# Block one's attention: scores issued two units ahead, behind the transposes, and a shorter VectorE chain

## The chip, the cores and the metric

The kernel runs on one core of one Trainium2 chip. The metric is the device time of one launch in microseconds (us). The engines named below are TensorE (PE in the profile, with PEld for its weight loads), VectorE (DVE), ScalarE (ACT), GpSimd (POOL) and SyncE (SP), which issues the weight loads from HBM.

## The reference

Two stacks of two layers each work on 256 tokens with 1024 channels. The change is in the first stack's token mixer. Each layer there has three kinds of softmax attention that a kernel computes side by side: compressed keys (15 of them, "cmp"), selected blocks and a sliding window (both over all earlier keys at this length, with a gate per head, "slc" and "win"), and attention with forget gates ("fox"). Cut to what the change touches:

```python
s_c = jnp.einsum('bqghd,bngd->bghqn', qb, kc)          # q was scaled by B_DH ** -0.5
p_c = _masked_softmax(s_c, cmp_end[None, :] <= t[:, None])

def _masked_softmax(logits, mask):
    m = jnp.max(logits, axis=-1, keepdims=True)
    p = jnp.where(mask, jnp.exp(logits - m), 0.0)
    return p / jnp.maximum(jnp.sum(p, axis=-1, keepdims=True), TINY)
# o = gate_cmp * o_cmp + gate_slc * o_slc + gate_win * o_win for the group heads; fox heads have no gate
```

The second stack (feed-forward layers, convolution, Fourier mixing and a latent attention) is untouched.

## The kernel before, in words

Nearly all of the time is weight products on TensorE. Weights stream from HBM through a ring of four slots; each 128x1024 tile is split in a high part (ScalarE, L773) and a low part (VectorE, L797), and three passes are made of it (L836, L840, L843).

The attention of block one is a stage of its own, once in each of the two layers, between the input products and the output product "wo". `units_block1` lists its 22 units: for each half of the queries (tt 0 and 1, 128 queries each) one cmp unit, then slc and win in turn four times, then two fox units. A unit is two heads. Its keys are 128 wide for tt 0 and 256 wide for tt 1. A unit has these steps, each with a semaphore that counts units:

- `unit_scores` (PE, L1114, or L1122/L1125 with a mask product L1131, for fox also L1130) writes two PSUM banks. It waits until the exponentials of the unit two before have been read out of those banks (`att_e`), and counts `att_s`.
- `unit_max` (DVE): two reductions L1201, a drain, and L1203 that writes the maximum negated and scaled; counts `att_m`. For cmp it is L1190 to L1196.
- `unit_exp` (ACT, L1254, L1249 for cmp): exponential with the row sum; counts `att_e`. It waits for the transposes of the unit two before, whose probability buffer it overwrites.
- `unit_norm` (DVE): reciprocal L1224, for slc and win the gate product L1228 with a drain, and two scalings of the probabilities L1232; counts `att_p`.
- `unit_turn` (PE, L1143, L1140 for cmp): transposes through the identity into bank 6; waits for `att_p` of its unit and for the copy of the unit before (`att_c`); counts `att_t`.
- `unit_copy` (ACT, L1266): bank 6 to SBUF; counts `att_c`.
- `unit_values` (PE, L1162, for slc also the compressed part L1156): values into bank 7; counts `att_v`. cmp has none.
- `unit_out` (ACT, L1273), for win and fox alone: bank 7 to SBUF; waits for `att_v`, counts `att_o`, for which the next slc or fox values wait.

Every engine takes its instructions in program order. In tick n PE does scores(n+1), one chunk of a modulation product ("ada", L934, in ticks 0 to 11 alone), turn(n-1) and values(n-2). DVE does max(n) and norm(n-1). ACT does exp(n), copy(n-1) and out(n-2). A few modulation steps (L915, L945, L955) lie between ticks. Behind the last out come the split of the attention output and the product wo.

Of the kernel before, what the change touches and what calls it, by code (L numbers as in the profile page):

```python
# [24 lines left out]
ALU = mybir.AluOpType  # L25
ACT = mybir.ActivationFunctionType
AX_X = mybir.AxisListType.X
# [10 lines left out]
DH = 64  # L38
# [527 lines left out]
def kernel_program(nc, streams, consts, params, x_cm, ctx_cm, out_cm, blocks=(1, 2)):  # L566
    with ExitStack() as stack:
# [100 lines left out]
        pr = pr_b.rearrange("p (u k) -> p u k", u=2)  # L668
# [12 lines left out]
        gate = gate_b.rearrange("p (t c) -> p t c", t=TT)  # L681
# [31 lines left out]
        s = Semaphores(sem)  # L713
# [361 lines left out]
        def units_block1(l):  # L1075
            out = []
            for tt in range(TT):
                out.append(Unit("cmp", tt))
                for g in range(2):
                    for j in range(2):  # L1080
                        out.append(Unit("slc", tt, g=g, j=j, first=True))
                        out.append(Unit("win", tt, g=g, j=j, last=True))
                for j in range(2):
                    out.append(Unit("fox", tt, j=j, first=True, last=True))
            base, obase = l * len(out), l * sum(x.last for x in out)
            vbase = l * sum(x.kind != "cmp" for x in out)
            o = v = 0
            for n, x in enumerate(out):
                x.u, x.o, x.v = base + n, obase + o, vbase + v
                x.kt = 1 if x.kind == "cmp" else x.tt + 1  # L1090
                x.keys = N_CMP if x.kind == "cmp" else x.kt * P
                x.scale = 1.0 if x.kind == "fox" else DH ** -0.5
                o += x.last
                v += x.kind != "cmp"
            return out
# [8 lines left out]
        def half_scores(x, hh):  # L1104
            return bank[(4, 5, 0, 2)[2 * (x.u % 2) + hh]]

        def unit_scores(pe, x):
            if x.u >= 2:
                pe.wait_ge(s.att_e, x.u - 1)
            q = slice(x.tt * P, (x.tt + 1) * P)  # L1110
            if x.kind == "cmp":
                for h in range(QH):
                    rows = slice(h % 2 * DH, h % 2 * DH + DH)
                    mm = pe.matmul(half_scores(x, h % 2)[:, h // 2 * N_CMP:(h // 2 + 1) * N_CMP], qr[rows, h // 2, q],  # L1114
                                   kcb[rows, h // 4 * N_CMP:(h // 4 + 1) * N_CMP], start=True, stop=True)
                mm.then_inc(s.att_s, 1)
                return
            for hh in range(2):
                rows = slice(hh * DH, hh * DH + DH)
                dst = half_scores(x, hh)[:, 0:x.keys]  # L1120
                if x.kind == "fox":
                    pe.matmul(dst, qkn[rows, 6 + x.j, q], qkn[rows, 8 + x.j, 0:x.keys], start=True, stop=False)  # L1122
                else:
                    key = kd[rows, x.g, 0 if x.kind == "slc" else 1, 0:x.keys]
                    pe.matmul(dst, qr[rows, 2 * x.g + x.j, q], key, start=True, stop=False)  # L1125
            for hh in range(2):
                dst = half_scores(x, hh)[:, 0:x.keys]
                if x.kind == "fox":
                    for st in range(x.kt):
                        pe.matmul(dst, fa[:, st, 2 * x.j + hh, q], gtk[:, st, 0:x.keys], start=False, stop=False)  # L1130
                mm = pe.matmul(dst[:, x.keys - P:x.keys], ident_b, causal_b, start=False, stop=True)  # L1131
            mm.then_inc(s.att_s, 1)
# [34 lines left out]

        def attention_pe(pe, l, units):
            unit_scores(pe, units[0])
            for n in range(len(units) + 2):  # L1170
                if n + 1 < len(units):
                    unit_scores(pe, units[n + 1])
                ada_pe(pe, l, TICK_ATT + n)
                if 1 <= n <= len(units):
                    unit_turn(pe, units[n - 1])
                if n >= 2:
                    unit_values(pe, units[n - 2])
                ada_fold_pe(pe, l, TICK_ATT + n)

        def unit_max(dve, x):  # L1180

            dve.wait_ge(s.att_s, x.u + 1)
            if x.u >= 2:
                dve.wait_ge(s.att_e, x.u - 1)
            if x.kind == "cmp":
                dst = c_sm[:, 0:heads_n].rearrange("p (h k) -> p h k", h=QH)
                pairs_of = c_sm[:, 0:heads_n].rearrange("p (m hh k) -> p m hh k", hh=2, k=N_CMP)
                for hh in range(2):
                    src = half_scores(x, hh)[:, 0:heads_n // 2].rearrange("p (m k) -> p m k", m=QH // 2)
                    dve.scalar_tensor_tensor(out=pairs_of[:, :, hh, :], in0=src, scalar=x.scale,  # L1190
                                             in1=cneg[:, x.tt, :].unsqueeze(1).broadcast_to([P, QH // 2, N_CMP]),
                                             op0=ALU.mult, op1=ALU.add)
                dve.drain()
                dve.tensor_reduce(c_max, dst, AX_X, ALU.max)
                dve.drain()
                dve.tensor_tensor(dst, dst, c_max.unsqueeze(2).broadcast_to([P, QH, N_CMP]),  # L1196
                                  ALU.subtract).then_inc(s.att_m, 1)
                return
            at = 2 * (x.u % 2)
            for hh in range(2):  # L1200
                dve.tensor_reduce(mx[:, at + hh:at + hh + 1], half_scores(x, hh)[:, 0:x.keys], AX_X, ALU.max)  # L1201
            dve.drain()
            dve.tensor_scalar(negmx[:, at:at + 2], mx[:, at:at + 2], -x.scale, None, ALU.mult).then_inc(s.att_m, 1)  # L1203

        def unit_norm(dve, x):

            dve.wait_ge(s.att_e, x.u + 1)
            at = 2 * (x.u % 2)
            if x.kind == "cmp":
                p_u = pr[:, x.u % 2, 0:heads_n].rearrange("p (h k) -> p h k", h=QH)  # L1210
                dve.tensor_tensor(p_u, p_u, cmask[:, x.tt, :].unsqueeze(1).broadcast_to([P, QH, N_CMP]), ALU.mult)
                dve.drain()
                dve.tensor_reduce(c_sum, p_u, AX_X, ALU.add)
                dve.drain()
                dve.tensor_scalar(c_sum, c_sum, TINY, None, ALU.max)
                dve.drain()
                dve.reciprocal(c_rcp, c_sum)
                dve.drain()
                dve.tensor_tensor(c_rcp, c_rcp, gate[:, x.tt, 0:QH], ALU.mult)
                dve.drain()  # L1220
                dve.tensor_tensor(p_u, p_u, c_rcp.unsqueeze(2).broadcast_to([P, QH, N_CMP]),
                                  ALU.mult).then_inc(s.att_p, 1)
                return
            dve.reciprocal(rcp[:, at:at + 2], smu[:, at:at + 2])  # L1224
            dve.drain()
            if x.kind != "fox":
                c0 = (8 if x.kind == "slc" else 16) + 4 * x.g + 2 * x.j
                dve.tensor_tensor(rcp[:, at:at + 2], rcp[:, at:at + 2], gate[:, x.tt, c0:c0 + 2], ALU.mult)  # L1228
                dve.drain()
            for hh in range(2):  # L1230
                c = slice(hh * x.keys, (hh + 1) * x.keys)
                last = dve.tensor_scalar(pr[:, x.u % 2, c], pr[:, x.u % 2, c], rcp[:, at + hh:at + hh + 1], None,  # L1232
                                         ALU.mult)
            last.then_inc(s.att_p, 1)

        def attention_dve(dve, l, units):
# [7 lines left out]
        def unit_exp(act, x):  # L1244
            act.wait_ge(s.att_m, x.u + 1)
            if x.u >= 2:
                act.wait_ge(s.att_t, x.u - 1)
            if x.kind == "cmp":
                act.activation(pr[:, x.u % 2, 0:heads_n], c_sm[:, 0:heads_n], ACT.Exp).then_inc(s.att_e, 1)  # L1249
                return  # L1250
            at = 2 * (x.u % 2)
            for hh in range(2):
                c = slice(hh * x.keys, (hh + 1) * x.keys)
                last = act.activation(pr[:, x.u % 2, c], half_scores(x, hh)[:, 0:x.keys], ACT.Exp, scale=x.scale,  # L1254
                                      bias=negmx[:, at + hh:at + hh + 1], accum_out=smu[:, at + hh:at + hh + 1])
            last.then_inc(s.att_e, 1)

# [675 lines left out]
        def block1_dve(dve, l):  # L1933
# [26 lines left out]

            dve.tensor_copy(qkg, param(f"qkg@{l}"))
            dve.drain()
            dve.tensor_scalar(qkg[:, 6:8], qkg[:, 6:8], DH ** -0.5, None, ALU.mult)
            dve.drain()
            dve.wait_ge(s.hn_rs, l + 1)
            for j in range(10):
# [1038 lines left out]
```

## Time and profile before

| | us |
|---|---|
| median of 3 runs | 2830.51 |
| lowest and highest | 2826.48, 2833.05 |
| profiled execution | 2829.12 |
| its span | 2827.3 |
| PE busy in it | 2741.4 (97%) |
| DVE busy in it | 1776.6 (63%) |
| ACT busy in it | 1065.5 (38%) |
| attention of layer 0, first to last weight load of the stage | 135.07 to 194.19 |
| attention of layer 1, the same | 529.43 to 588.16 |

The profile is one execution. Its own time is 1.8 us more than its span, which is from the first instruction to the last. A busy share says how much of the span an engine had an instruction in work. Ends of matmuls are modelled, so in the attention stage the start times of the weight loads (PEld) tell the order and pace of TensorE best.

### The profile page before, as it was taken

What the parts mean: (1) busy time and instruction counts of PE and PEld (TensorE: products, weight loads), DVE (VectorE), ACT (ScalarE), POOL (GpSimd) and SP (SyncE); (2) the same over time, 40 slices, a digit from 0 to 9 for tenths busy, and PEclk for the clock granted to TensorE, in tenths of its full rate; (3) what the DMA queues carried; (4) which work ended last, traced back from release to release, by engine and by line L of the source; (5) the groups of instructions that cost most, each with busy time, mean ns of one, the idle gap of its engine ahead of it and who ended that gap; (6) DMA issues with size and microseconds to landing.
All of it is one profiled execution on the core that took longest, in us unless ns stands there. A gap on an engine that the chain in (4) does not pass through costs nothing.

```text
span 2827.3 us, 45215 instructions
## 1 busy us (share of the span) xinstructions
PE 2741.4 (97%) x16508; PEld 2334.7 (83%) x16508; DVE 1776.6 (63%) x3023; ACT 1065.5 (38%) x1704; POOL 192.0 (7%) x184
## 2 busy tenths in 40 slices
PE   8999999999999999999999999999999999899998
PEld 8669999589988888775777788888788888689998
DVE  7466656566676565587675665555665557756665
ACT  5356444366342221325434322222322214554443
POOL 0000000000000000032213000000000000134000
PEclk9999999999999999999999999999999999999999
DMA  5535544635544433321432244433344433244554
GB/s 194 197 117 196 183 165 156 216 131 184 180 142 141 148 139 132 115 72 64 137 133 66 90 142 148 141 135 131 130 142 148 142 126 120 83 129 156 168 177 157
DMA packets 118649, 401.16 MB, mean 142 GB/s; under 512 B 12928, under 2 KB 20992, under 8 KB 118144
## 3 DMA queue, kind: packets, MB, share of 16 engines
q1 hardware_dynamic: 115408, 392.48, 41.0%
q10 hardware_dynamic: 3120, 7.07, 0.7%
q8 instruction: 76, 1.25, 0.2%
q14 instruction: 45, 0.37, 0.0%
HBM read 398.45 MB, written 1.05 MB: 141 GB/s over the span
## 4 chain that ended last, share of the span: by engine, by line
PE 86%; DVE 5%; issue 4%; DMA 2%; ACT 1%; POOL 1%; DVEq 1%; ACTq 0%; POOLq 0%; SPq 0%
PE bank L836 24%; PE bank L843 24%; PE bank L840 24%; PE bank L1595 2%; DMA ring<-weights 1%; PE bank L2088 1%; PE bank L2447 1%; PE bank L2444 1%; PE bank L2441 1%; DVE work L2209 1%; DVE hn_lo L1069 1%; PE bank L934 1%; DVE w_lo L797 1%; POOL w_lo L797 1%; PE bank L1326 1%
## 5 line engine op out<-in xcount | busy, mean ns | idle before, releaser
L773 ACT ACTIVATE w_hi<-ring 128x1024 fp32r<-128x1024 f32 (+1 forms) x548 | 572.1, 1045 | 1158.3 <-DMA ring<-weights 1157.7
L797 DVE TENSOR_TENSOR w_lo<-ring,w_hi 128x1024 fp32r<-128x1024 f32 (+1 forms) x538 | 658.9, 1226 | 526.6 <-ACT w_hi L773 522.1
L840 PE MATMUL bank<-hn_hi,w_hi 128*128 128x256 f32 (+1 forms) x2848 | 896.9, 333 | 0.0
L843 PE MATMUL bank<-hn_lo,w_hi 128*128 128x256 f32 (+1 forms) x2848 | 896.7, 333 | 0.0
L840 PEld LDWEIGHTS bank<-hn_hi,w_hi 128*128 128x128 f32 x2848 | 542.2, 190 | 52.2
L843 PEld LDWEIGHTS bank<-hn_lo,w_hi 128*128 128x128 f32 x2848 | 542.2, 190 | 52.1
L836 PE MATMUL bank<-hn_hi,w_lo 128*128 128x256 f32 (+1 forms) x2848 | 570.4, 336 | 10.3 <-DVE w_lo L797 7.3
L836 PEld LDWEIGHTS bank<-hn_hi,w_lo 128*128 128x128 f32 x2848 | 453.7, 190 | 71.3 <-issue 11.5
L840 PE MATMUL bank<-hid_hi,w_hi 128*128 128x512 f32 (+1 forms) x704 | 248.7, 362 | 0.0
L843 PE MATMUL bank<-hid_lo_a,w_hi 128*128 128x512 f32 (+1 forms) x640 | 226.2, 362 | 0.0
L964 DVE SCALAR_TENSOR_TENSOR conds<-ring,con 128x1024 f32<-128x1024 f32 x106 | 131.3, 1239 | 58.8 <-DMA ring<-weights 42.0
L836 PE MATMUL bank<-hid_hi,w_lo 128*128 128x512 f32 (+1 forms) x704 | 156.5, 363 | 0.0
L840 PEld LDWEIGHTS bank<-hid_hi,w_hi 128*128 128x128 f32 x704 | 132.9, 189 | 20.6
L836 PEld LDWEIGHTS bank<-hid_hi,w_lo 128*128 128x128 f32 x704 | 121.9, 189 | 20.7 <-DVE w_lo L797 0.2
L843 PEld LDWEIGHTS bank<-hid_lo_a,w_hi 128*128 128x128 f32 x640 | 120.8, 189 | 18.7
L966 DVE SCALAR_TENSOR_TENSOR ring<-ring,con 128x1024 f32<-128x1024 f32 x106 | 131.5, 1241 | 0.0
L840 PE MATMUL bank<-up_hi,w_hi 128*128 128x256 f32 x512 | 125.6, 283 | 0.0
L843 PE MATMUL bank<-up_lo,w_hi 128*128 128x256 f32 x512 | 125.6, 283 | 0.0
L2797 DVE SCALAR_TENSOR_TENSOR hid<-work,par,hid 128x512 f32<-128x512 f32 (+1 forms) x180 | 117.4, 707 | 4.8
L2861 POOL MEMSET work<- 128x1716 f32 x2 | 3.1, 1528 | 1492.4 <-issue 790.1
L840 PEld LDWEIGHTS bank<-up_hi,w_hi 128*128 128x128 f32 x512 | 98.3, 192 | 0.0
L843 PEld LDWEIGHTS bank<-up_lo,w_hi 128*128 128x128 f32 x512 | 98.3, 192 | 0.0
(350 smaller groups left out, 3127.7 us busy)
## 6 DMA issues: line engine op xcount, KB each, us to landing
ring<-weights SPq DMA_DIRECT2D x694, 512.0 KB, 3.3
ring<-weights SPq DMA_DIRECT2D x32, 384.0 KB, 3.0
ring<-weights SPq DMA_DIRECT2D x32, 256.0 KB, 2.9
ring<-weights SPq DMA_DIRECT2D x28, 192.0 KB, 2.3
con<-consts ACTq DMA_DIRECT2D x1, 2063.0 KB, 9.5
con<-consts ACTq DMA_DIRECT2D x1, 1088.0 KB, 5.4
res<-ctx_cm ACTq DMA_DIRECT2D x1, 1024.0 KB, 7.7
con<-params ACTq DMA_DIRECT2D x1, 1024.0 KB, 11.0
```

What stands on the lines that cost most here:

```text
L773: act.activation(w_hi[:, slot, 0:w], ring[slot][:, 0:w], ACT.Copy).then_inc(s.w_hi, 1)
L797: eng.tensor_tensor(w_lo[slot][:, 0:w], ring[slot][:, 0:w], w_hi[:, slot, 0:w].bitcast(F32), ALU.subtract).then_inc(s.w_lo, 1)
L836: pe.matmul(dst, w_lo[slot][:, k * P:(k + 1) * P], x_hi(k), start=(start and k == order[0]), stop=False)
L840: pe.matmul(dst, high, x_hi(k), start=False, stop=False)
L843: return pe.matmul(dst, high, x_lo(k), start=False, stop=(stop and k == order[-1]))
L934: mm = pe.matmul(ada_bank(h)[rows, :], cs[:, k, COND_AT - 2 * q:COND_W - 2 * q], ring[slot][:, i * 4 * P:(i + 1) * 4 * P], start=(q == 0 a ...
L964: dve.scalar_tensor_tensor(out=conds[:, :], in0=ring[slot][:, :], scalar=1.0, in1=crow[:, 0:D], op0=ALU.mult, op1=ALU.mult, accum_out=to[: ...
L966: dve.scalar_tensor_tensor(out=ring[slot][:, :], in0=ring[slot][:, :], scalar=1.0, in1=crow[:, D:2 * D], op0=ALU.mult, op1=ALU.mult, accum ...
L1069: last = dve.scalar_tensor_tensor(out=hn_lo[:, k, t], in0=sq[:, k, t], scalar=modulation(l)[:, SHIFT[which], k, c:c + 1], in1=hn_hi[:, k, ...
L1326: mm = pe.matmul(bank[6 + hh][:, c0:c0 + P], keys, queries, start=True, stop=True)
L1595: mm = pe.matmul(bank[2 * parity(lin, g)][:, q], sq[:, k, q], ring[slot_of(lin, g, 0)][:, k * P:(k + 1) * P], start=(k == 0), stop=(k == K ...
L2797: last = dve.scalar_tensor_tensor(out=dst, in0=src, scalar=taps[:, m, k:k + 1], in1=dst, op0=ALU.mult, op1=ALU.add)
```

## The change

Three things change. On TensorE the scores of a unit are issued two units ahead where they were issued one ahead, and their place in a tick moves from ahead of the ada chunk to between the transposes and the values. On VectorE the reduction itself writes the negated maximum, so that L1203 and one drain go; to this end the score scale moves into the query gain, and ScalarE's exponential loses its scale factor. And the gate of slc and win becomes a second factor of the two scalings, so that L1228 and its drain go. The first gain step (L1963) covers six columns instead of two.

```diff
         def attention_pe(pe, l, units):
             unit_scores(pe, units[0])
+            unit_scores(pe, units[1])
             for n in range(len(units) + 2):
-                if n + 1 < len(units):
-                    unit_scores(pe, units[n + 1])
                 ada_pe(pe, l, TICK_ATT + n)
                 if 1 <= n <= len(units):
                     unit_turn(pe, units[n - 1])
+                if n + 2 < len(units):
+                    unit_scores(pe, units[n + 2])
                 if n >= 2:
                     unit_values(pe, units[n - 2])
                 ada_fold_pe(pe, l, TICK_ATT + n)
...
             for hh in range(2):
-                dve.tensor_reduce(mx[:, at + hh:at + hh + 1], half_scores(x, hh)[:, 0:x.keys], AX_X, ALU.max)
-            dve.drain()
-            dve.tensor_scalar(negmx[:, at:at + 2], mx[:, at:at + 2], -x.scale, None, ALU.mult).then_inc(s.att_m, 1)
+                last = dve.tensor_reduce(negmx[:, at + hh:at + hh + 1], half_scores(x, hh)[:, 0:x.keys], AX_X, ALU.max,
+                                         negate=True)
+            last.then_inc(s.att_m, 1)
...
             dve.reciprocal(rcp[:, at:at + 2], smu[:, at:at + 2])
             dve.drain()
-            if x.kind != "fox":
-                c0 = (8 if x.kind == "slc" else 16) + 4 * x.g + 2 * x.j
-                dve.tensor_tensor(rcp[:, at:at + 2], rcp[:, at:at + 2], gate[:, x.tt, c0:c0 + 2], ALU.mult)
-                dve.drain()
             for hh in range(2):
                 c = slice(hh * x.keys, (hh + 1) * x.keys)
-                last = dve.tensor_scalar(pr[:, x.u % 2, c], pr[:, x.u % 2, c], rcp[:, at + hh:at + hh + 1], None,
-                                         ALU.mult)
+                share = rcp[:, at + hh:at + hh + 1]
+                if x.kind == "fox":
+                    last = dve.tensor_scalar(pr[:, x.u % 2, c], pr[:, x.u % 2, c], share, None, ALU.mult)
+                else:
+                    c0 = (8 if x.kind == "slc" else 16) + 4 * x.g + 2 * x.j + hh
+                    last = dve.tensor_scalar(pr[:, x.u % 2, c], pr[:, x.u % 2, c], share, gate[:, x.tt, c0:c0 + 1],
+                                             ALU.mult, ALU.mult)
             last.then_inc(s.att_p, 1)
...
-                last = act.activation(pr[:, x.u % 2, c], half_scores(x, hh)[:, 0:x.keys], ACT.Exp, scale=x.scale,
+                last = act.activation(pr[:, x.u % 2, c], half_scores(x, hh)[:, 0:x.keys], ACT.Exp,
                                       bias=negmx[:, at + hh:at + hh + 1], accum_out=smu[:, at + hh:at + hh + 1])
...
-            dve.tensor_scalar(qkg[:, 6:8], qkg[:, 6:8], DH ** -0.5, None, ALU.mult)
+            dve.tensor_scalar(qkg[:, 2:8], qkg[:, 2:8], DH ** -0.5, None, ALU.mult)
```

## Rows read from the trace of the kernel before

**Rows 1.** The page: busy time (share) by engine, and the chain that ended last.

```profile
PE 2741.4 (97%) x16508; PEld 2334.7 (83%) x16508; DVE 1776.6 (63%) x3023; ACT 1065.5 (38%) x1704; POOL 192.0 (7%) x184
PE 86%; DVE 5%; issue 4%; DMA 2%; ACT 1%; POOL 1%; DVEq 1%; ACTq 0%; POOLq 0%; SPq 0%
```

**Rows 2.** Stretches: length, PE, PEld, DVE, ACT, POOL busy (x), PEclk, DMA share, GB/s.

```profile
150.00:160.00 10.00, 10.00 (x74) 5.47 (x76) 4.47 (x25) 4.22 (x20) 0.00 (x0) 1.00 0.57 178
180.00:190.00 10.00, 9.79 (x74) 7.06 (x74) 5.16 (x22) 5.03 (x18) 0.00 (x0) 1.00 0.00 1
```

**Rows 3.** Timeline, layer 0, an ada tick: start, us, engine, line, out<-in [idle <-releaser].

```profile
146.52 0.20 PEld L1143 LDWEIGHTS bank<-con,work 128*128 128x128 f32 x2 [0.84 <-issue]
...
146.89 0.20 PEld L1162 LDWEIGHTS bank<-work 128*64 128x64 f32 x4 [0.17 <-issue]
...
147.26 0.30 PEld L1125 LDWEIGHTS bank<-hid 64*128 64x128 f32 x4 [0.17 <-issue]
...
147.90 0.14 PEld L934 LDWEIGHTS bank<-ring,conds 128*32 128x32 f32 x4
...
148.88 0.20 PEld L1143 LDWEIGHTS bank<-con,work 128*128 128x128 f32 x2 [0.84 <-issue]
```

**Rows 4.** Timeline, layer 0, one win tick of tt 1, PE's loads and ACT.

```profile
178.09 0.30 PEld L1125 LDWEIGHTS bank<-hid 64*128 64x128 f32 x4 [0.17 <-issue]
...
178.79 0.42 PEld L1143 LDWEIGHTS bank<-con,work 128*128 128x128 f32 x4
...
179.38 0.42 PEld L1162 LDWEIGHTS bank<-work 128*64 128x64 f32 x8 [0.17 <-issue]
...
179.49 0.60 ACT L1266 ACTIVATE work<-bank 128x512 f32<-128x512 f32 x1 [0.60 <-PE bank L1143]
...
179.97 0.30 PEld L1125 LDWEIGHTS bank<-hid 64*128 64x128 f32 x4 [0.17 <-issue]
...
180.09 0.28 ACT L1273 ACTIVATE work<-bank 128x128 f32<-128x128 f32 x1
...
180.26 0.47 ACT L1254 ACTIVATE work<-bank,small 128x256 f32<-128x256 f32 x1
...
181.06 0.21 ACT L1254 ACTIVATION_READ_ACCUMULATOR work<-bank,small 128x1 f32 x1
181.10 0.42 PEld L1143 LDWEIGHTS bank<-con,work 128*128 128x128 f32 x4 [0.38 <-DVE work L1232]
```

**Rows 5.** Timeline, layer 0, DVE in one slc tick of tt 1.

```profile
174.63 0.76 DVE L1201 TENSOR_REDUCE small<-bank 128x1 f32<-128x256 f32 x2
...
175.47 0.17 DVE L1203 TENSOR_SCALAR small<-small 128x2 f32<-128x2 f32 x1
...
175.78 0.16 DVE L1228 TENSOR_TENSOR small<-small 128x2 f32<-128x2 f32 x1
...
176.02 0.61 DVE L1232 TENSOR_SCALAR work<-work,small 128x256 f32<-128x256 f32 x2
```

**Rows 6.** Timeline, layer 0, fox scores of tt 1 and two waits of the tail.

```profile
182.49 0.30 PEld L1122 LDWEIGHTS bank<-hid 64*128 64x128 f32 x4 [0.17 <-issue]
...
185.08 0.42 PEld L1143 LDWEIGHTS bank<-con,work 128*128 128x128 f32 x4
...
190.91 0.66 PE L1143 MATMUL bank<-con,work 128*128 128x128 f32 x4 [0.60 <-DVE work L1232]
...
194.22 0.66 PE L1162 MATMUL bank<-work 128*64 128x128 f32 x8 [0.66 <-ACT work L1273]
```

**Rows 7.** Lines 1356 and 1358: one scaling with two factors, one with one.

```profile
L1356 DVE TENSOR_SCALAR work<-work,small x4: 406/408/414, 27.9 to 423.4; 128x256 f32<-128x256 f32 x4
L1358 DVE TENSOR_SCALAR work<-work,small x4: 345/346/349, 28.2 to 423.7; 128x256 f32<-128x256 f32 x4
```

**Rows 8.** Timeline, layer 1: first and last weight load of the attention.

```profile
529.43 1.00 PEld L1114 LDWEIGHTS bank<-small,hid 64*128 64x128 f32 x16 [2.33 <-issue]
...
588.16 0.45 PEld L1162 LDWEIGHTS bank<-work 128*64 128x64 f32 x8 [0.86 <-ACT work L1266]
```

More of the change, by code:

```diff
@@ L1091, in units_block1 @@
                 x.keys = N_CMP if x.kind == "cmp" else x.kt * P
-                x.scale = 1.0 if x.kind == "fox" else DH ** -0.5
                 o += x.last
@@ L1189, in unit_max @@
                     src = half_scores(x, hh)[:, 0:heads_n // 2].rearrange("p (m k) -> p m k", m=QH // 2)
-                    dve.scalar_tensor_tensor(out=pairs_of[:, :, hh, :], in0=src, scalar=x.scale,
+                    dve.scalar_tensor_tensor(out=pairs_of[:, :, hh, :], in0=src, scalar=1.0,
                                              in1=cneg[:, x.tt, :].unsqueeze(1).broadcast_to([P, QH // 2, N_CMP]),
```

## The prediction

> **What bounds the kernel now.** I read the page first, for the busy shares and the chain that ended last. TensorE is busy for 97% of the span and carries 86% of the chain [rows 1]. So an edit is worth what it does to TensorE's pace, and time saved on another engine is worth something only where TensorE waits for it. Next I read the stage, 135.07 to 194.19 in layer 0, by stretches: from 150 to 160 TensorE is busy all the time, from 180 to 190 for 9.79 of 10 us, with the clock at its full level (2.4 GHz) in both; the DMA engines are idle in the second stretch, so the ring is full and no weight is late [rows 2]. Whatever the stage gains or loses therefore passes on to wo. Last I read the timeline by the starts of weight loads. A tick with an ada chunk and without the compressed part lasts 2.36 us (146.52 to 148.88), of which the chunk holds PE for 0.98 (147.90 to 148.88) [rows 3]. A tt 1 tick without a chunk is scores 0.70 (178.09 to 178.79), transposes 0.59 (to 179.38) and values 0.59 (to 179.97), 1.88 in all [rows 4]; one with the compressed part has some 0.23 more, and fox scores last 2.59 (182.49 to 185.08) [rows 6]. TensorE's true waits are few: 0.38 for the scaling at 181.10 [rows 4], then 0.60 and 0.66 in the tail [rows 6].
>
> **VectorE's part.** L1203 starts at 175.47, 0.84 after the reductions, and L1224 follows it by 0.08; L1228 sits between at 175.78, and L1232 follows 0.24 behind it [rows 5]. The change takes away about 0.23 ahead of the exponential and 0.24 ahead of the scaling. The second factor adds time: 408 against 346 ns for the same size, 0.06 for each of two scalings [rows 7]. Net, VectorE has 0.35 us less in a slc or win unit. That the reduction costs the same with the sign turned no row shows; it is the same pass over the same elements, and I take nothing for it, between 0 and one L1203 (0.17, [rows 5]) in a unit. The two edits are worth what TensorE waited for VectorE. The gain on six columns and ScalarE's missing factor change no count and no width: 0, hidden in any case behind rows of 0.17.
>
> **How I sum the order of the work.** I laid the 22 units out. Each step starts at the later of its engine's turn and its semaphores: PE steps as above, an exponential of tt 1 takes 1.04 (180.26 to 181.06 and its second read of 0.21), a copy 0.60 with the next step 0.49 after its start, an out 0.28 with the next step 0.17 after (180.09 to 180.26); transposes release the copy 0.70 after they start (178.79 to 179.49), values release the out 0.71 after (179.38 to 180.09) [rows 4]. For the order before, this gives the last two waits in the right places (the transposes at 190.98, where the trace has 190.91 [rows 6]) and 59.6 us from the first scores to the end of the last values' issue; the trace has 135.07 to 194.22 and 0.42 for the eight loads. So it may be used for the order after, with an error of some 0.5 us.
>
> **What the move adds: tile switches.** PE's queue shows 0.17 of idle with no releaser whenever the shape of the array tile changes: 64 rows after values, 64 columns after transposes, and none between L1131 and the transposes, which both use the whole array [rows 3, 4]. In ticks 12 to 19, which have no chunk, the order scores, transposes, values has three changes (one lies inside the scores). The order transposes, scores, values has four. In chunk ticks both orders have five. With one around tick 13's fold I count 57 changes before and 66 after: 9 x 0.17 = 1.5 us a layer. The switches from transposes to scores and from the mask product to values are in no row; the bounds are 0 and 0.27 each. I take 0.17, since every other change shows it. The Trainium skill, TensorEngine Tiling (Array Packing), section Tiling Modes, states that a change of tiling mode drains TensorE. By that rule the move costs these switches, and without it none; the rows have it as the 0.17.
>
> **What the move adds: a wait.** Scores(n+2) write the banks of unit n, so they wait for exp(n). They used to be scores(n+1) waiting for exp(n-1), long done. Behind them on PE now stand values(n-2); for those stands out(n-2) on ScalarE; and behind out(n-2), in program order, exp(n+1), for which scores(n+3) wait. So where unit n-2 is win or fox there is a closed chain. Counting from the end of exp(n): scores 0.70, switch 0.17, values release the out at 0.87 + 0.71 = 1.58, exp(n+1) starts at 1.75 and ends at 1.75 + 1.04 = 2.79, 2.82 with its semaphore. PE meanwhile is through scores, values (0.87 + 0.59 = 1.46) and turn(n) (2.04), and then holds scores(n+3), with values behind them, for 0.78. In chunk ticks the 0.98 of the chunk covers this, and tt 0's exponential is shorter: 0.26 in one tick. Laid out over the stage, scores(14) wait 1.01 and scores(15) 1.25 (a modulation copy stands ahead of exp(13) as well), scores(18) and scores(20) 0.78 each: 3.8 us.
>
> **The sum.** Waits of PE before, by the same layout: 1.78 up to tick 18, the most for norm (0.40 and 0.50 behind cmp, 0.19, 0.25, 0.44), all but 0.28 of which the longer lead and the shorter VectorE chain remove; and 1.76 in the tail. After: 0.28 and 0.26 early, 3.82 for the exponentials, 1.96 in the tail, where scores(21) are delayed through out(17) and turn(20) waits 0.73. That is 6.3 against 4.0, +2.3 a layer; with the switches 1.5, +3.8. Layer 1 has the same stage (529.43 to 588.16, [rows 8]), so +7.7 us. The profiled execution has 2829.12 with a span of 2827.3; it would have 2836.8. That execution is 1.4 below the median of 2830.51, so on the median it is 2838.2, and I say 2838.
>
> **The rivals.** (a) *The outs don't bind, not slower.* If the values release the out before the scores matter, or the exponentials keep their lead, the 3.8 goes and the 1.3 that turn waited for norm stays won. Laid out with outs that never wait, the stage takes 58.7: -0.9 a layer, 2828.6. It speaks for it that in the 2.36 us ticks ScalarE has long pauses. It speaks against it that in tt 1 out and exponential follow within 0.17 [rows 4]. It decides where values plus out come less than 0.78 later than I have them. (b) *One of the two new switches is free.* 61.1 or 61.8 in place of 63.5: +1.5 or +2.1 a layer, 2833.4 to 2834.8. (c) *Both free and the outs don't bind, faster.* 55.3: -4.4 a layer, 2821.8; then TensorE's issue alone is the bound, and the 0.17 that rows show at other changes speaks against it. (d) *The new switches cost more*, 0.27: 66.6, +7 a layer, 2844.4. (e) That only VectorE's edits act, were the order without effect, gives 58.2 in the layout, -1.4 a layer, 2827.7; it is in (a)'s share.
>
> **How the numbers follow.** A measurement of this kernel can tell about 0.2%, 5.7 us, from no change. The forecast (both switches paid, closed chain) has 0.46; with 0.5 us for the layout's error either way and the same for the exponential's semaphore it holds +5.7 to +10. (b) has 0.25, (a) with (e) 0.14, (c) 0.06, (d) 0.09. Slower by over 0.2%: 0.46 + 0.09 = 0.55. Within: 0.25 + 0.14 = 0.39. Faster: 0.06. The range leaves out (c) and (d), 0.15 together, and runs from just under (a) to the top of the forecast with the spread of the medians: 2828 to 2842.
>
> **What would show it.** In the profile after: attention stages some 3.8 us longer each; in the tt 1 ticks PE idle before L1125 and L1122, released by ACT L1254, where before it was L1143 waiting for DVE L1232; L1273 of a tt 1 tick starting 1.4 or more after L1266 instead of 0.60; 0.17 of unreleased idle ahead of L1125 behind L1143, and ahead of L1162 or L1156 behind L1131; DVE with 40 fewer L1203 and 32 fewer L1228, and L1232 some 60 ns longer with two factors. The prediction is wrong if L1125 waits for nothing in ticks 12 to 19, or if the stage ends before 59 us.

## The result and the profile after

The changed kernel takes 2843.34 us (median of 7 runs, 2838.34 to 2847.35) against 2830.51 (7 runs): a ratio of 1.0043 with a 95% interval of 1.0029 to 1.0057, so 12.8 us slower. The direction was forecast; the size was 7.7, and the time lies 1.3 us above the range.

The page of the changed kernel, its busy times and the chain that ended last, to be read beside [rows 1]:

```profile
PE 2751.6 (97%) x16508; PEld 2341.4 (82%) x16508; DVE 1772.1 (62%) x2951; ACT 1067.0 (38%) x1704; POOL 191.8 (7%) x184
PE 86%; DVE 4%; issue 4%; ACT 2%; DMA 2%; POOL 1%; DVEq 1%; ACTq 0%; SPq 0%; POOLq 0%
```

TensorE has the same instructions and is busy 10 us longer; ScalarE's share of the chain has gone from 1% to 2%. VectorE has 72 instructions fewer. None of this tells where the time went. The two attention stages tell it, each from the first weight load of its scores to the end of the last one of its values (columns as in [rows 2]). First the two of the kernel before, by the same limits, then the two of the changed kernel:

```profile
135.07:194.64 59.57, 56.55 (x438) 32.47 (x438) 37.21 (x166) 32.53 (x119) 0.00 (x0) 1.00 0.40 141
529.43:588.61 59.18, 56.64 (x438) 32.46 (x438) 37.16 (x166) 32.62 (x119) 0.00 (x0) 1.00 0.40 138
138.73:205.41 66.68, 60.85 (x438) 34.63 (x438) 34.28 (x130) 31.68 (x119) 0.00 (x0) 0.95 0.36 123
541.25:607.37 66.12, 59.34 (x438) 32.93 (x438) 34.12 (x130) 31.76 (x119) 0.00 (x0) 0.97 0.36 124
```

The stages of the changed kernel are 7.1 and 6.9 us longer. The span is 16.6 longer in this execution; 3.7 of it lie ahead of the first stage (its start was 135.07), where the order of the attention plays no part yet; I put them down to the scatter of single executions. The forecast had +3.9 a stage. The third column from the right shows what comes on top: the mean granted clock is 0.95 and 0.97 of full, where the stages before had 1.00. Half of the time spent at half speed is lost, so 0.05 x 66.68 = 3.3 us were lost to the clock in the first stage, and 0.03 x 66.12 = 2.0 us in the second. The first stage without that is 63.4 us long; the layout by hand had 63.5.

The second stage is another case. Its loads wait for weights in the first ticks, the clock is low right behind that wait, and it is full again from 552 to the end of the stage:

```profile
547.90 0.14 PEld L934 LDWEIGHTS bank<-ring,conds 128*32 128x32 f32 x4 [1.47 <-DMA ring<-weights]
```

```profile
548.00:550.00 2.00, 2.00 (x8) 0.37 (x8) 0.00 (x0) 0.00 (x0) 0.00 (x0) 0.59 0.71 277
550.00:552.00 2.00, 2.00 (x11) 0.80 (x10) 0.79 (x4) 1.08 (x5) 0.00 (x0) 0.56 0.72 229
```

That stretch lies ahead of ticks 12 and 13 and is not behind the waits described next. It also comes in executions of versions that are not slower (see the experiments), so the 6.9 us of this stage are not all owed to the change.

The waits are where they were forecast, in both layers. Layer 0, ticks 12 and 13, TensorE's weight loads:

```profile
172.16 0.14 PEld L1139 LDWEIGHTS bank<-con,work 128*120 128x120 f32 x1 [0.17 <-DVE work L1221]
173.52 0.30 PEld L1124 LDWEIGHTS bank<-hid 64*128 64x128 f32 x4 [1.22 <-ACT work L1255]
...
174.37 0.20 PEld L1161 LDWEIGHTS bank<-work 128*64 128x64 f32 x4
174.74 0.42 PEld L1142 LDWEIGHTS bank<-con,work 128*128 128x128 f32 x4 [0.17 <-issue]
176.58 0.51 PEld L1124 LDWEIGHTS bank<-hid 64*128 64x128 f32 x4 [1.43 <-ACT work L1255]
```

The scores L1124 wait 1.22 and 1.43 for the exponential L1255 (1.01 and 1.25 were forecast, besides the switch of 0.17). In the last row a group of four loads takes 0.51 where it took 0.30 three rows above. The clock in these microseconds:

```profile
176.00:178.00 2.00, 1.42 (x7) 0.77 (x7) 0.90 (x3) 1.93 (x8) 0.00 (x0) 0.58 0.00 0
178.00:180.00 2.00, 2.00 (x12) 2.00 (x11) 0.21 (x3) 0.00 (x0) 0.00 (x0) 0.50 0.00 0
180.00:182.00 2.00, 2.00 (x11) 1.02 (x9) 1.62 (x8) 1.26 (x4) 0.00 (x0) 0.50 0.00 0
```

TensorE stood still for two waits of over a microsecond close together. From about 176.2, within the second wait, it was granted the lower of its two levels (1.2 GHz), and kept it until about 183, though it was busy all the time from 178 to 182. The closed chain is seen best in tick 16 (layer 0, TensorE's loads and ScalarE's steps):

```profile
184.04 0.30 PEld L1124 LDWEIGHTS bank<-hid 64*128 64x128 f32 x4 [0.17 <-issue]
...
184.89 0.41 PEld L1161 LDWEIGHTS bank<-work 128*64 128x64 f32 x8
...
185.47 0.42 PEld L1142 LDWEIGHTS bank<-con,work 128*128 128x128 f32 x4 [0.17 <-issue]
...
185.59 0.28 ACT L1274 ACTIVATE work<-bank 128x128 f32<-128x128 f32 x1 [0.85 <-PE bank L1161]
185.77 0.47 ACT L1255 ACTIVATE work<-bank,small 128x256 f32<-128x256 f32 x1
...
186.83 0.30 PEld L1124 LDWEIGHTS bank<-hid 64*128 64x128 f32 x4 [0.94 <-ACT work L1255]
```

Scores at 184.04, values behind them at 184.89, the out L1274 0.70 later after 0.85 of idling on ScalarE, the exponential behind it, and 0.94 of waiting before the next scores. VectorE's edits came out as read from [rows 5, 7]. These are groups of the changed kernel (count, busy us, mean ns, idle before): the reduction costs the 352 ns of before with its sign turned; the two-factor scaling L1233 is 377 on the average of both widths, against 317 for the one-factor form.

```profile
L1201 DVE TENSOR_REDUCE small<-bank 128x1 f32<-128x128 f32 (+1 forms) x80 | 24.8, 352 | 29.7 <-PE bank L1130 29.7
L1233 DVE TENSOR_SCALAR work<-work,small 128x128 f32<-128x128 f32 (+1 forms) x64 | 21.4, 377 | 2.5
L1230 DVE TENSOR_SCALAR work<-work,small 128x128 f32<-128x128 f32 (+1 forms) x16 | 4.4, 317 | 0.6
```

### The profile page after: what moved, and what is told of

Read it like the earlier page. It is cut to its first block, busy times and chain, and to the rows that moved or that the text cites. A ratio compares the mean times of both kernels' runs of the same rounds, so it can differ in the third digit from the quotient of the medians.

```text
span 2843.9 us, 45071 instructions
## 1 busy us (share of the span) xinstructions
PE 2751.6 (97%) x16508; PEld 2341.4 (82%) x16508; DVE 1772.1 (62%) x2951; ACT 1067.0 (38%) x1704; POOL 191.8 (7%) x184
## 3 DMA queue, kind: packets, MB, share of 16 engines
q8 instruction: 76, 1.25, 0.2%
## 4 chain that ended last, share of the span: by engine, by line
PE 86%; DVE 4%; issue 4%; ACT 2%; DMA 2%; POOL 1%; DVEq 1%; ACTq 0%; SPq 0%; POOLq 0%
PE bank L836 24%; PE bank L843 24%; PE bank L840 24%; PE bank L1596 2%; DMA ring<-weights 2%; PE bank L2089 1%; PE bank L2448 1%; PE bank L2442 1%; PE bank L2445 1%; DVE work L2210 1%; DVE hn_lo L1069 1%; PE bank L934 1%; POOL w_lo L797 1%; PE bank L1327 1%; PE bank L2118 1%
## 6 DMA issues: line engine op xcount, KB each, us to landing
con<-consts ACTq DMA_DIRECT2D x1, 2063.0 KB, 10.2
```

## The experiments

The theory (A) is that the order of TensorE's work makes a closed chain of waits, and that the clock falls behind these waits. In short diffs the changed kernel is the one being edited unless it says otherwise.

**One part alone: VectorE's edits.** The scores go back to one ahead, ahead of the chunk; the rest of the change stays.

```diff
-            unit_scores(pe, units[1])
             for n in range(len(units) + 2):
+                if n + 1 < len(units):
+                    unit_scores(pe, units[n + 1])
                 ada_pe(pe, l, TICK_ATT + n)
...
-                if n + 2 < len(units):
-                    unit_scores(pe, units[n + 2])
```

> VectorE's two edits alone, with the scores one ahead and in their old place. Theory A (the loss is the order of TensorE's work): the stage shrinks from 59.6 to about 58.2 us in each layer, and the kernel takes 2.8 us less than the one before, with L1203's drain and L1228's gone and two-factor scalings some 60 ns longer. Rival B (the loss comes from the shorter VectorE chain, for instance from the reductions that write the sign turned): slower than before, by up to the 12.8 us of the whole change.

Measured: 2828.83 (11 runs) against 2831.56 (29), ratio 0.9992 (0.9983 to 1.0000): 2.7 us less, at the edge of what can be told from nothing. The stages:

```profile
137.21:195.46 58.25, 56.01 (x438) 32.43 (x438) 33.70 (x130) 32.37 (x119) 0.00 (x0) 1.00 0.42 144
531.17:592.01 60.84, 57.67 (x438) 32.79 (x438) 33.54 (x130) 32.38 (x119) 0.00 (x0) 0.97 0.40 135
```

The first is the 58.2 of the layout. The second has a wait of 1.6 us for weights in its first ticks and a short stretch of lower clock right behind it (0.03 x 60.84 = 1.8 us), as the second stage of the changed kernel had. B is out: VectorE's part does not cost time.

**The other part alone: the order.** The kernel before, with TensorE's order of the change.

> The new order of TensorE alone, with VectorE's steps as before. Theory A: 63.6 us a stage where the clock stays full, as waits of about 1.2 and 1.4 us before the scores of ticks 12 and 13 and of about 0.9 in ticks 16 and 18; +8 us from these alone, and with the clock falling behind them in some executions +8 to +14 against before. Rival B: about the time of before.

Measured: 2844.12 (5 runs), ratio 1.0045 (1.0032 to 1.0058), 12.6 us more: the whole loss. Its first stage is 66.68 us long, with 6.8 us at half speed behind tick 13. Its second stage:

```profile
537.09:604.97 67.88, 62.14 (x438) 35.19 (x438) 37.74 (x166) 31.91 (x119) 0.00 (x0) 0.92 0.35 120
...
572.00:574.00 2.00, 1.62 (x14) 0.77 (x12) 1.57 (x6) 0.92 (x3) 0.00 (x0) 1.00 0.00 0
574.00:576.00 2.00, 1.19 (x5) 0.54 (x6) 0.94 (x4) 2.00 (x9) 0.00 (x0) 0.53 0.02 4
576.00:578.00 2.00, 2.00 (x13) 2.00 (x12) 0.00 (x0) 0.16 (x2) 0.00 (x0) 0.50 0.04 8
```

Here the clock fell at 574, in the second of the two waits, and stayed down for 10.2 us; half of that, 5.1 us, went with it, and the stage without them is 62.8 long.

**The chain opened on TensorE.** The scores stay two ahead, behind the values.

```diff
+                if n >= 2:
+                    unit_values(pe, units[n - 2])
                 if n + 2 < len(units):
                     unit_scores(pe, units[n + 2])
-                if n >= 2:
-                    unit_values(pe, units[n - 2])
```

> The whole change, but the scores two ahead stand behind the values in each tick, not ahead of them. Theory A (scores, values, out and the next exponential form a closed chain, and a ninth more tile switches): the chain is open and the switches are those of before, so a stage takes 58.2 us, -2.8 against before and some -15 against the changed kernel, and TensorE waits nowhere for an exponential over 0.3 us. Rival C (having scores two ahead at all is what costs, since the banks are those of the unit whose exponential is not done): the waits for the exponentials stay and the time is that of the changed kernel, +12.

Measured: 2827.50 (12 runs), ratio 0.9989 (0.9980 to 0.9998): 4.1 us under the kernel before and some 16 under the changed one. Both stages are 57.7 us long, at full clock:

```profile
136.47:194.16 57.69, 56.08 (x438) 32.33 (x438) 33.50 (x130) 32.33 (x119) 0.00 (x0) 1.00 0.41 141
528.94:586.64 57.70, 56.09 (x438) 32.33 (x438) 33.52 (x130) 32.34 (x119) 0.00 (x0) 1.00 0.40 141
```

And a tick of its timeline (TensorE's loads, ScalarE's steps):

```profile
175.52 0.42 PEld L1161 LDWEIGHTS bank<-work 128*64 128x64 f32 x8 [0.17 <-issue]
176.11 0.30 PEld L1124 LDWEIGHTS bank<-hid 64*128 64x128 f32 x4 [0.17 <-issue]
176.22 0.28 ACT L1274 ACTIVATE work<-bank 128x128 f32<-128x128 f32 x1
176.40 0.47 ACT L1255 ACTIVATE work<-bank,small 128x256 f32<-128x256 f32 x1
...
176.81 0.42 PEld L1142 LDWEIGHTS bank<-con,work 128*128 128x128 f32 x4
```

The out L1274 starts 0.70 after the values as ever, but the scores run beside it, and the transposes follow the mask product L1130 with no switch. C is out: two ahead is not in itself what costs.

**The chain opened on ScalarE.** TensorE's order is the change's, but the copy of a finished output stands behind the next exponential.

```diff
                     unit_exp(act, units[n])
+                if 3 <= n <= len(units):
+                    unit_out(act, units[n - 3])
                 if 1 <= n <= len(units):
                     unit_copy(act, units[n - 1])
-                if n >= 2:
+                if n >= len(units):
                     unit_out(act, units[n - 2])
```

> The changed kernel, with ScalarE's copy of a finished output put behind the next exponential, not ahead of it; TensorE's order is as in the change. Theory A: the exponential no longer stands behind the values, the waits of ticks 12 to 19 go, and a stage takes 59.0 us, -1.2 against before, though the nine added tile switches stay. Rival D (the place of the scores costs by itself, through the switches or the longer ticks): at least +8 against before stays.

Measured: 2830.47 (11 runs), ratio 0.9996 (0.9987 to 1.0004), 1.1 us under the kernel before: the loss is gone though no instruction of TensorE has moved. Stages of 60.27, with 1.6 of waiting for weights, and 60.56, with 0.5 of it and 0.03 of the clock. In the timeline:

```profile
178.06 0.30 PEld L1124 LDWEIGHTS bank<-hid 64*128 64x128 f32 x4 [0.17 <-issue]
178.16 0.60 ACT L1267 ACTIVATE work<-bank 128x512 f32<-128x512 f32 x1 [0.71 <-PE bank L1142]
178.66 0.47 ACT L1255 ACTIVATE work<-bank,small 128x256 f32<-128x256 f32 x1
...
178.91 0.42 PEld L1161 LDWEIGHTS bank<-work 128*64 128x64 f32 x8
...
179.61 0.28 ACT L1274 ACTIVATE work<-bank 128x128 f32<-128x128 f32 x1
180.08 0.30 PEld L1124 LDWEIGHTS bank<-hid 64*128 64x128 f32 x4 [0.17 <-issue]
```

The exponential starts at 178.66, before the values have even been issued, and the out follows at 179.61. The scores at 180.08 wait for nothing but the switch. D, which wanted at least +8, is out, and this also fixes which link closed the chain: the out in ScalarE's queue.

**The clock: work in the waits.** A product nobody reads is set into the waits of ticks 12 and 13.

```diff
+                if n in (12, 13):
+                    pe.wait_ge(s.ada_out, 2 * l + 1)
+                    pe.matmul(bank[1][:, :], ident, const(1, "gtk"), start=True, stop=True)
                 if n + 2 < len(units):
                     unit_scores(pe, units[n + 2])
```

> The changed kernel, with one product of 128x512 fp32 (0.86 us, into a bank nobody reads, so no result changes) set ahead of the scores of ticks 12 and 13, inside the two longest waits for an exponential. Theory A (in the stages the clock falls because TensorE idles there, and this is the second part of the loss): the waits of those ticks shrink by 0.85 each in the trace, no step is later, the clock stays full from tick 12 to the stage's end in both layers, a stage takes 63.5 us where the weights come in time, and the time falls by 2 to 5 us against the changed kernel, to some +8 to +10 against before. Rival F (the clock falls for another reason, such as the kind of work, or the excess over +7.7 is spread elsewhere): the half-speed stretch behind tick 13 stays and the time is that of the changed kernel or above it, +12 to +14.

Measured: 2839.97 (5 runs), ratio 1.0034 (1.0021 to 1.0048), +9.3 us. Its stages are 64.08 and 65.11 us long; the clock is full behind tick 13 in both, and the second has 3.4 us at half speed in its first ticks. Run once more, beside the changed kernel itself:

> The changed kernel once more, unedited, beside the one with the products in the waits. Theory A: waits of 1.2 and 1.4 us in ticks 12 and 13 in both layers; a half-speed stretch of 5 to 8 us behind them in at least one of the two stages; +10 to +14 against before. A stage is 63.5 us plus half of its time at the lower level plus its waits for weights. Rival F: stages longer than that with the clock full.

> The version with the product in the waits of ticks 12 and 13, once more. Theory A: clock full behind tick 13 in both layers again, and a time below that of the changed kernel in the same job by 2 to 5 us, +8 to +10 against before. Rival F: the same time as the changed kernel.

Measured: the changed kernel 2844.01 (5 runs), 1.0037 (1.0023 to 1.0051), +12.3; with the products 2839.51 (7 runs), 1.0031 (1.0020 to 1.0043), +7.8. Twice the version with more work on TensorE is the faster one by median, by 3.4 and 4.5 us, but the intervals overlap, so the medians alone don't settle it. The traces say more of the mechanism. First the version with products, its loads in layer 0, then its stages in the repetition:

```profile
170.00 0.35 PEld L1176 LDWEIGHTS bank<-con,con 128*128 128x128 f32 x2
171.36 0.30 PEld L1124 LDWEIGHTS bank<-hid 64*128 64x128 f32 x4 [1.00 <-ACT work L1258]
...
172.97 0.30 PEld L1176 LDWEIGHTS bank<-con,con 128*128 128x128 f32 x2
174.42 0.30 PEld L1124 LDWEIGHTS bank<-hid 64*128 64x128 f32 x4 [1.15 <-ACT work L1258]
```

```profile
139.28:203.80 64.52, 59.49 (x442) 33.04 (x442) 34.35 (x130) 31.76 (x119) 0.00 (x0) 1.00 0.38 130
539.27:604.00 64.73, 59.58 (x442) 33.02 (x442) 34.28 (x130) 31.77 (x119) 0.00 (x0) 1.00 0.38 129
```

The scores come at the same distance as before, 3.06 apart (171.36 and 174.42, against 173.52 and 176.58); the products L1176 delay nothing. The idle times in the brackets are those of the loading side, during which the product runs. Both stages keep the full clock; they hold 1.4 and 1.5 of waiting for weights. Now the repetition of the changed kernel, its two stages and a stretch of the second:

```profile
137.32:200.70 63.38, 57.82 (x438) 32.53 (x438) 34.28 (x130) 31.83 (x119) 0.00 (x0) 1.00 0.39 129
536.10:605.72 69.62, 62.42 (x438) 34.72 (x438) 34.31 (x130) 31.76 (x119) 0.00 (x0) 0.93 0.35 120
578.00:580.00 2.00, 2.00 (x12) 1.67 (x13) 1.10 (x7) 0.34 (x3) 0.00 (x0) 0.54 0.00 0
580.00:582.00 2.00, 2.00 (x12) 1.12 (x12) 1.45 (x5) 1.31 (x5) 0.00 (x0) 0.50 0.00 0
```

The first stage kept its clock and is 63.38 us long, which is the layout's 63.5. The second was at half speed for 10.2 us and lost 5.1: 3.4 of the 10.2 lie in its first ticks, behind a wait for weights, and 6.8 behind tick 13. So the same waits sometimes lead to the fall and sometimes don't.

**Work in all four waits.** The same, with `n in (12, 13, 16, 18)`.

> The same product in ticks 12, 13, 16 and 18. Theory A: as with two, since the waits of 0.94 in ticks 16 and 18 stood alone and were followed by full clock; +8 to +10 against before. If the single waits matter too, 1 to 3 us less than with two. Rival F: +12 to +14.

Measured: 2843.27 (5 runs), 1.0045 (1.0031 to 1.0059), +12.6. This was expected at +8 to +10. Its trace has stages of 64.31 and 65.45, 0.2 and 0.3 longer than with two products, the clock full behind tick 13 in both; so the further 3.3 us of the median are not in the stages of the execution that was profiled. The interval overlaps that of the version with two. Whether the two further products cost something that the profiled execution does not show, or five runs fell high, is open. By its median this version has not gained on the changed kernel at all, so the remedy is less sure than the pair of runs above makes it look.

**The clock in all runs.** Only one or two executions of each version were profiled, but every run has its span and its mean granted clock. The span times what the clock lacks to 1 is the time given up to the clock (an upper bound, since a low clock costs nothing while TensorE waits), and the rest is the span at full clock. In means, with the uncertainty of each mean:

| | runs | given up to the clock | at full clock |
|---|---|---|---|
| kernel before | 55 | 30.4 (0.5) | 2799.0 (0.3) |
| order of the change (the changed kernel and the order alone) | 17 | 33.6 (1.1) | 2807.6 (0.7) |
| the same order with products in the waits (two or four) | 17 | 30.7 (0.7) | 2808.3 (0.6) |

The order costs 8.6 us at full clock and 3.2 us more of the clock; with the products the second is gone and the first stays. The 3.2 is uncertain by 1.2, and the changed kernel by itself (12 runs) has 32.9, so the size of the clock's part is known only as a few microseconds.

**The lead alone.** Values first, on the kernel before, with VectorE's steps as they were.

> Scores two ahead behind the values, with VectorE's steps as before. Theory A: the chain is open, no switch is added, and the longer lead removes little; the layout gives 59.5 us a stage, no change against before (within 1 us), and the gain of the version with the values first comes from VectorE's edits. Rival G (the longer lead itself gains): 2 us or more under before.

Measured: 2830.35 (11 runs), 0.9999 (0.9990 to 1.0008), 0.3 us less. The lead in the open place gains nothing that can be measured; the gain of the version with the values first comes with VectorE's edits. G asked for 2 us or more; the median is against it, though the interval reaches down to 2.8 us less.

## Why the prediction was right in direction and short in size

- **TensorE is the bound, and other engines' time counts only where it waits.** Right. VectorE's 40 products and 32 gate products less were worth 2.7 us by the medians, 2.8 in the layout; the interval of that measurement ends at no gain.
- **The costs of VectorE's edits.** Right: the reduction kept its 352 ns, and the second factor costs 60 ns by both rows.
- **Tile switches.** Right, and the two that no row showed are there: 0.17 of unreleased idle between L1142 and L1124 (at 184.04), and from the mask product L1130 it takes 0.22 to the values L1161 (184.67 to 184.89), where it takes 0.07 to the compressed part L1155, which has the whole array's columns:

```profile
184.67 0.11 PEld L1130 LDWEIGHTS bank<-mask_parts 128*128 128x128 bf16 x2 [0.33 <-issue]
184.89 0.41 PEld L1161 LDWEIGHTS bank<-work 128*64 128x64 f32 x8
...
187.46 0.11 PEld L1130 LDWEIGHTS bank<-mask_parts 128*128 128x128 bf16 x2 [0.33 <-issue]
187.53 0.30 PEld L1155 LDWEIGHTS bank<-work 120*128 120x128 f32 x2
```

  That is 0.15 for the second new switch. The trace of before has such a step at another place: in [rows 3] the L934 at 147.90, which has 32 columns, starts 0.22 after the mask product's loads (147.68) and shows no idle in brackets, so not every change shows the 0.17 as such. This is the rule of the Trainium skill, TensorEngine Tiling (Array Packing), section Tiling Modes, that a change of mode drains TensorE; the trace agrees, with these 0.17 and 0.15. Rival (b) is out. With the out moved on ScalarE the added switches stay, and the time is that of before; it is 3.0 us above the version with the values first, whose VectorE edits are the same, where the layouts have 1.6 between them, and the intervals overlap.
- **The closed chain.** Right in place and size: waits of 1.22, 1.43, 0.94 and 0.94 on the loading side (0.17 of each is the switch), forecast 1.01, 1.25, 0.78 and 0.78. Both ways to open it removed the loss, so it is shown and not only argued. The tail's wait came as well. Rivals (a), (c) and (e) are out.
- **The sum.** Here is the step that failed: it took TensorE's clock as given. I had read the full level in [rows 2] for both stretches and carried it over to an order that puts two idle times of over a microsecond close together. The stage at full clock is 63.4 us, as laid out; the term put at nothing is what the clock takes. The six stages of the change's order that were profiled without products (two executions of the changed kernel, one of the order alone) have a fall behind tick 12 or 13 in four: about 6.8 us at half speed in three of them and 10.2 in one. That is 3.4 x 3 + 5.1 = 15.3 us lost in six stages, 2.6 a stage, 5.1 a kernel. With the 7.7 of the waits and switches it makes 12.8, which is what was measured; that this agrees so well is luck. The means over all runs have 3.2 for the clock and 8.6 for the waits and switches, 11.8 together. What stands behind the clock as the cause is that none of the six stages with products in the waits had such a fall. If the products did nothing and the stages were independent, four falls in twelve stages would all land among the six without them about 3 times in 100. Why the fall comes in one stage and not in the next stays open.
- **An addition in the sum.** The waits listed for the order before are 1.78 and 1.76, 3.5 in all and not 4.0. From the listed terms the change comes to +2.8 a layer, +4.3 with the switches and +8.6 us in all; the 7.7 is that of the two stage lengths of the layout, 63.5 and 59.6. The runs at full clock have 8.6, uncertain by 0.8, and don't tell the two apart. With 8.6 the forecast would have been 2839, still inside the range and short of what was measured.
- **The range.** It went to 2842 with the spread of the medians at its top. Rival (d), dearer switches, reached further but was the wrong mechanism. With 5.1 us for the clock in each of the two stages, the most that one stage lost behind its waits, the top would have been at 2838 + 2 x 5.1 = 2848.

The version with the values first beats both kernels, by 4.1 us and by some 16.

## What to carry to other kernels

When a step on one engine is moved past another, follow the semaphores once around: scores, values, a copy on ScalarE and the exponential queued behind it were each harmless in the order before, and closed to a ring only in this one. Moving the scores behind the values, or the copy behind the exponential, opened it. And where a sum puts new idle time on TensorE, give the clock a term of its own, with a range from nothing up: here it was nothing in some stages and up to 5.1 us in one, some 3 to 5 us a kernel beside the 8 to 9 of the waits and switches.

## What the runs showed of the hardware

- In the profiled stages TensorE spent 3.4, 6.8 or 10.2 us at the lower level, or none. Behind two waits of 1.2 and 1.4 us, whose ends are 3.1 us apart, it fell in four stages out of six; behind the waits of 0.94 in ticks 16 and 18, 5.1 us apart, in none.
- The lower level outlasted the waits. From 178 to 182 in the changed kernel TensorE was busy all the time and still at half speed.
- In seven of the eleven profiled executions, whatever the order, the second layer's stage had a stretch of 3.4 us at the lower level in its first ticks, near a wait for weights of 0.7 to 1.8 us on the loading side; among the four without it were the kernel before and the one with the values first. In the first layer's stage weights were waited for as long as 1.19 and 1.56 us, and the clock stayed full there. Whether the wait for weights is the cause was not tried, and some of the scatter between executions may come from it.
